# Sparse and forgetting attention written anew: split operands, both token tiles in one bank, rows scaled before the turning

## What is computed

```python
    g = jax.nn.sigmoid(gate.astype(jnp.float32)).reshape(B, T, H, 3)
    o = g[..., 0:1] * o_cmp + g[..., 1:2] * o_slc + g[..., 2:3] * o_win
    return o.astype(h.dtype).reshape(B, T, H * dh) @ w_out
...
    scale = dh ** -0.5
    c = jnp.cumsum(logf, axis=1).transpose(0, 2, 1)
...
        s = jnp.einsum('bqhd,bkhd->bhqk', q[:, lo:hi], k[:, :hi]).astype(jnp.float32) * scale
        s = s + c[:, :, lo:hi, None] - c[:, :, None, :hi]
...
        p = jax.nn.softmax(jnp.where(causal, s, NEG_INF), axis=-1)
        outs.append(jnp.einsum('bhqk,bkhd->bqhd', p.astype(v.dtype), v[:, :hi]))
```

## Time and profile before

| | |
|---|---|
| runs | 3452.91, 3432.66, 3448.34 us; median 3448.34 |
| profiled execution | 3428.43 us, of which the trace's span is 3426.6 |
| busy | PE 3150.3 us (92%), DVE 2056.8 (60%), ACT 1526.5 (45%), POOL 537.9 (16%) |
| chain that ended last | PE 53%, DVE 4%, ACT 1%, POOL 1% |
| granted PE clock, mean | 0.880 of full speed |
| DMA | 134 GB/s over the span, the busiest queue 39.1% of 16 engines |

### The profile page before, as it was taken

How to read it: one execution, slowest core, us unless ns; L and a number is a source line. 1 busy time by engine, 2 the same in 40 slices (tenths; PEclk the granted TensorE clock), 3 DMA queues, 4 the chain that set the end, 5 groups by cost and what they waited for, 6 DMA issues and landing times.

```text
span 3426.6 us, 61848 instructions
## 1 busy us (share of the span) xinstructions
PE 3150.3 (92%) x21774; PEld 2946.0 (86%) x21774; DVE 2056.8 (60%) x4479; ACT 1526.5 (45%) x3283; POOL 537.9 (16%) x590
## 2 busy tenths in 40 slices
PE   7189689999999989798899999999899999999998
PEld 7188679999999867787799999998777799976898
DVE  7948967676776552588676666666422356431465
ACT  5352345555555432423455555554322355531454
POOL 4522680000100110127700000002100010100100
PEclk9589899999999996899999999999655699885799
DMA  4035216666665430352265555554300045430254
GB/s 133 21 113 171 86 55 222 214 231 207 227 225 184 133 111 1 105 173 87 71 220 184 184 183 184 183 184 167 105 1 1 25 144 183 135 104 0 93 184 141
DMA packets 140749, 460.07 MB, mean 134 GB/s; under 512 B 15776, under 2 KB 33568, under 8 KB 140464
## 3 DMA queue, kind: packets, MB, share of 16 engines
q1 hardware_dynamic: 135120, 436.75, 39.1%
q0 software_dynamic: 5472, 21.30, 2.1%
HBM read 448.48 MB, written 9.50 MB: 134 GB/s over the span
## 4 chain that ended last, share of the span: by engine, by line
PE 53%; DVE 4%; ACT 1%; POOL 1%; issue 1%; DVEq 0%; DMA 0%; POOLq 0%; ACTq 0%; SPq 0%
PE banks L769 37%; PE banks L1077 4%; PE banks L1075 3%; PE banks L1096 2%; PE banks L915 2%; PE banks L892 1%; PE banks L1086 1%; PE banks L788 1%; PE banks L1014 1%; POOL x_lo L2012 1%; DVE arena L1667 0%; DVE arena L1680 0%; DVE arena L1633 0%; DVE arena L1626 0%; DVE arena L1627 0%
## 5 line engine op out<-in xcount | busy, mean ns | idle before, releaser
L454 DVE TENSOR_TENSOR w_lo<-ring,w_hi 128x512 fp32r<-128x512 f32 x1464 | 1026.3, 707 | 764.7 <-ACT w_hi L447 758.3
L447 ACT ACTIVATE w_hi<-ring 128x512 fp32r<-128x512 f32 x1464 | 917.9, 631 | 967.1 <-PE banks L769 920.1
L769 PE MATMUL banks<-x_hi,w_hi 128*128 128x256 f32 (+2 forms) x3136 | 913.6, 291 | 57.4 <-POOL x_lo L2012 22.0
L769 PE MATMUL banks<-x_lo,w_hi 128*128 128x256 f32 (+2 forms) x3136 | 905.5, 289 | 0.0
L769 PE MATMUL banks<-x_hi,w_lo 128*128 128x256 f32 (+2 forms) x3136 | 903.1, 288 | 0.0
L769 PE MATMUL banks<-gated_hi,w_hi 128*128 128x256 f32 x2560 | 728.2, 284 | 10.2 <-DVE gated_lo L1760 10.0
L769 PE MATMUL banks<-gated_hi,w_lo 128*128 128x256 f32 x2560 | 727.5, 284 | 0.0
L769 PE MATMUL banks<-gated_lo,w_hi 128*128 128x256 f32 x2560 | 726.2, 284 | 0.0
L769 PEld LDWEIGHTS banks<-x_hi,w_hi 128*128 128x128 f32 x3136 | 613.1, 196 | 67.0 <-issue 40.6
L769 PEld LDWEIGHTS banks<-x_lo,w_hi 128*128 128x128 f32 x3136 | 613.6, 196 | 0.7
L769 PEld LDWEIGHTS banks<-x_hi,w_lo 128*128 128x128 f32 x3136 | 614.0, 196 | 0.0
(11 more groups left out here) (234 smaller groups left out, 3238.9 us busy)
## 6 DMA issues: line engine op xcount, KB each, us to landing
ring<-in_peer_v SPq DMA_DIRECT2D x256, 512.0 KB, 3.5
ring<-in_peer_u SPq DMA_DIRECT2D x192, 512.0 KB, 3.4
arena<-in_peer_u SPq DMA_DIRECT2D x64, 512.0 KB, 3.6
ring<-in_mlp_up SPq DMA_DIRECT2D x64, 512.0 KB, 3.3
ring<-in_mlp_down SPq DMA_DIRECT2D x64, 512.0 KB, 3.3
ring<-w_peer_query SPq DMA_DIRECT2D x32, 512.0 KB, 3.3
ring<-w_fox_proj SPq DMA_DIRECT2D x24, 512.0 KB, 3.4
ring<-w_nsa_proj SPq DMA_DIRECT2D x20, 512.0 KB, 3.4
```

The costliest lines, as they stand in the source:

```text
L447: act.activation(w_hi[:, hn % SPLITS], raw_half(hn), ACT.Copy).then_inc(hi_ready, 1)
L454: dve.tensor_tensor(w_lo[:, hn % SPLITS], raw_half(hn), w_hi[:, hn % SPLITS].bitcast(F32), ALU.subtract)\
L769: mm = pe.matmul(out, w_at(w), x, start=start and j == 0, stop=stop and j == 2, skip_group_check=True)
```

## The change

The attentions of nsa and fox get a new set of functions, `attend_pairs` on four engines and `pair_units`; the first attention (diff) keeps `attend`. A unit is now one head with one set of keys and both token tiles: its scores, 2 x 256 columns, fill one PSUM bank. nsa has 32 such units (8 pairs of heads x 2 x 2 branches), fox 16. q, k, v, masks, decay and the turned probabilities are split into float32r parts. DVE (128 columns) and POOL (256 columns) scale the rows by gate and 1/sum before PE turns them. The values, padded with zeros to 128 columns, are the stationary operand, so the output comes out feature by token and goes split to `x_hi` and `x_lo`; `turn_out` and two barriers per attention are gone, and `proj_keep` waits chunk by chunk. The compressed branch is done for all heads at once, before the first units.

The stages, and PE's part:

```diff
-    ("nsa_attn", dict()),
-    ("turn_out", dict()),
+    ("nsa_attn", dict(joined=True)),
     ("proj_keep", dict(chunks=8, gi=1, squares=NC, joined=True)),
...
+            def attend_pairs(s, units):
...
+                def cmp_scores():
+                    for t in range(NT):
+                        for j in range(8):
+                            o = banks[:, 6, t * SEQ + j * 32:t * SEQ + (j + 1) * 32]
+                            ts = slice(t * P, (t + 1) * P)
+                            for n, (q, k) in enumerate(((q_hi, kc_hi), (q_lo, kc_hi), (q_hi, kc_lo))):
+                                mm = pe.matmul(o, q[:, j, ts], k[:, j // 4], start=n == 0, stop=n == 2, skip_group_check=True)
+                    mm.then_inc(cmp_scored, 1)
...
+                def scores(u):
+                    un = units[u]
+                    if u >= 2:
+                        pe.wait_ge(pair_exp, p0 + u - 1)
+                    o, rows = banks[:, u % 2, :], slice(64 * un["b"], 64 * un["b"] + 64)
+                    pe.matmul(o, ident_r[:, :], mask_r[:, :], start=True, stop=False, skip_group_check=True)
+                    if fox:
+                        sel = ident_r[0:16, un["head"]:un["head"] + 1].broadcast_to([16, P])
+                        for part in range(2):
+                            pe.matmul(o, sel, decay[:, part], start=False, stop=False, skip_group_check=True)
+                    for t in range(NT):
+                        ts = slice(t * P, (t + 1) * P)
+                        for n, (q, k) in enumerate(((q_hi, k_hi), (q_lo, k_hi), (q_hi, k_lo))):
+                            mm = pe.matmul(o[:, t * SEQ:(t + 1) * SEQ], q[rows, un["chunk"], ts], k[rows, un["k"]],
+                                           start=False, stop=t == 1 and n == 2, skip_group_check=True)
...
+                def weigh(u):
+                    pe.wait_ge(pair_lo, p0 + u + 1)
...
+                    for kt, (vh, vl) in enumerate(un["v"]):
+                        at = SEQ if kt == 0 else 0
+                        ph, pl = (pair_pT[:, u % 2, i, at:at + SEQ] for i in range(2))
+                        for n, (v, p) in enumerate(((vh, ph), (vh, pl), (vl, ph))):
+                            mm = pe.matmul(o, v, p, start=first, stop=un["last"] and kt == 1 and n == 2, skip_group_check=True)
...
+                for u in range(len(units) + 3):
+                    if u < len(units):
+                        scores(u)
+                    if u == 2 and not fox:
+                        cmp_turn()
+                    if 2 <= u < len(units) + 2:
+                        turn(u - 2)
+                    if u >= 3:
+                        weigh(u - 3)
```

ACT's order of a unit:

```diff
+                for u in range(len(units) + 4):
+                    if u < len(units):
+                        exps(u)
...
+                    if 2 <= u < len(units) + 2:
+                        round_turned(u - 2)
+                    if u >= 4 and units[u - 4]["last"]:
+                        round_out(u - 4)
```

DVE's:

```diff
+                for u in range(len(units) + 4):
+                    if u < len(units):
+                        maxima(u)
+                    if 1 <= u < len(units) + 1:
+                        scale_rows(u - 1)
...
+                    if 2 <= u < len(units) + 2:
+                        turned_rest(u - 2)
+                    if u >= 4 and units[u - 4]["last"]:
+                        out_rest(u - 4)
```

POOL's:

```diff
+            def attend_pairs(s, units):
+                for u in range(len(units)):
+                    pool.wait_ge(pair_coef, s["p0"] + u + 1)
+                    row = pair_p[:, u % 3, SEQ:2 * SEQ]
+                    pool.tensor_scalar(row, row, pair_coef_[:, u % 3, 1:2], None, ALU.mult).then_inc(pair_scaled_pool, 1)
```

```diff
-        POOL_GROUPS = range(8, GROUPS_OF_TWO)
+        POOL_GROUPS = [g for g in range(8, GROUPS_OF_TWO) if g % 6 != 5]
...
-                    pool.tensor_tensor(hit4, hit4, tk["code"].unsqueeze(2).broadcast_to([P, HEADS, TOPK, NCAND]), ALU.mult)\
-                        .then_inc(hit_ready, 1)
+                    for hd in range(HEADS):
+                        code = tk["code"][:, hd].unsqueeze(1).broadcast_to([P, TOPK, NCAND])
+                        ins = pool.tensor_tensor(hit4[:, hd], hit4[:, hd], code, ALU.mult)
+                    ins.then_inc(hit_ready, 1)
```

More of the change, by code:

```diff
@@ L548, in nsa_rope_dst, with nsa_rope_parts, pair_units @@
         def nsa_rope_dst(m):
-            return qT[:, m] if m < 8 else (kcT, ksT, kwT)[(m - 8) // 2][:, m % 2]
+            return kcT[:, m - 8] if m in (8, 9) else rope_out[:, m % 3]
+        NSA_SPLIT = [m for m in range(14) if m not in (8, 9)]
+        def nsa_rope_parts(m):
+            return (q_hi[:, m], q_lo[:, m]) if m < 8 else (k_hi[:, m - 10], k_lo[:, m - 10])
+        def pair_units(kind):
+            units = []
+            if kind == "fox_attn":
+                for pr in range(8):
+                    for b in range(2):
+                        units.append(dict(chunk=pr, b=b, k=pr, first=b == 0, last=b == 1, head=2 * pr + b,
+                                          v=[(fox_v_hi[:, kt, pr, b], fox_v_lo[:, kt, pr, b]) for kt in range(2)]))
+            else:
+                for j in range(8):
+                    pair = j // 4
+                    for b in range(2):
+                        for i in range(2):
+                            units.append(dict(chunk=j, b=b, k=2 * i + pair, first=b + i == 0, last=b + i == 2,
+                                              gate=3 * (4 * (2 * pair + b) + j % 4) + 1 + i,
+                                              v=[(nsa_v_hi[:, kt, i, pair, b], nsa_v_lo[:, kt, i, pair, b]) for kt in range(2)]))
+            return units
         def block_rows(eng, kv):
@@ L1408, in rope @@
                     follow(split_hi, act, n0 + m)
+                    if beside is not None:
+                        beside(m)
                     act.wait_ge(half_used, 2 * (n0 + m + 1))
```

440 lines of the change are left out of this document (328 added, 112 removed).

## The result

The changed kernel takes 3232.85 us (median of four runs, 3221.49 to 3244.31), beside 3448.32 for the kernel before: ratio 0.9393, 95% interval 0.935 to 0.9435. The forecast was 3223, with a range of 3180 to 3284. On the profiled executions the gain is smaller than on the medians: 3428.43 became 3240.0, where 3202.9 was forecast.

A forecast was written before the change was run, and what follows sets the result against it. PE at half clock was taken to bound nsa's attention. Gains of 123.9 (nsa), 82.6 (fox) and 20 (experts), less 1, make 225.5 us: profiled 3428.4 becomes 3202.9, median 3448.3 becomes 3223, range 3180 to 3284.

The forecast's parts named there:

- the loop over ACT's rounding: New attention units: DVE maxima, ACT exponentials, ACT rounding, DVE rest in turn, 2.82 us; 2.95 nsa, 3.05 fox with output's rest.
- above PE's 2.02 and 2.49 at full clock: New units: the loop outlasts PE's work at full clock, priced at 2.02 us per nsa unit and 2.49 per fox unit.
- The compressed scores: Nsa attention's start: 48 matmuls with new weights at half clock, 48 x 0.214 = 10.3 us.
- I expect it back within the first units, then kept: Both new attentions: PE's clock returns to full within the first units and stays, as new units send more columns per microsecond.
- The ends of 0.8 and 1.2: PE's price for matmuls on 64 and 16 partitions: the full-height price, with ends at 0.8 and 1.2 of it.
- the later casts and shifts of the same tile meet the last pieces, so I take 9: Choice of experts, layer 0: cutting POOL's product into eight pieces gets back 9 us (2 to 11).
- no gain in the choice of experts: Rival: casts meet piece after piece and DVE takes over as bound of the one-hot groups; 3243 us, chance 0.06.
- Half clock: Rival: PE stays at 0.50 in both attentions and ends last, 45 us more, 3268; chance 0.20.
- Held port at the row scaling: Rival: DVE's row scaling in the units waits for POOL's, issued at the same moment; 16 us more, 3239; chance 0.11.
- Serial units: Rival "slower": attention units do not overlap and PE stays at half clock, 8.0 to 8.1 us per unit; 3472; chance 0.03.
- POOL's cover: New units: POOL's scaling of 256 columns, taken as 1.1 us, is hidden with some 1.5 us of cover before ACT's rounding.
- nothing in the change bears on that distance: Whole kernel: the profiled execution lies 19.9 us below the runs' median, and this distance was carried over unchanged.

The follow-up runs named there:

- experiment 1: Changed kernel with ACT rounding the turned piece of the unit two back before this unit's exponentials, not behind them; ratio 0.9375 to the kernel before.
- experiment 8: Changed kernel with DVE scaling all 384 columns, POOL's scaling and PE's wait for it gone; nsa 112.1 us, fox 73.7 us.
- experiment 4: Changed kernel with 40 matmuls of 512 columns into an unread bank filling PE's wait at the start of the compress stage; ratio 0.9409.
- experiment 10: Changed kernel with ACT's rounding first and fox's two decay matmuls per unit left out; fox 46.4 us, its full-clock units 2.34 us on average.
- experiment 5: Kernel before with only POOL's product in the choice of experts cut into eight pieces; 3422.65 us in one run.
- experiment 6: Kernel before with only the POOL one-hot groups cut from 120 to 100; 3429.53 us in one run, groups 120.9 and 120.1 us.
- experiment 2: Changed kernel with POOL's row scaling doubled by an extra multiplication by 1.0; nsa 119.1 us against 112.5, fox units 3.08 against 2.985.
- experiment 3: Changed kernel with 18 matmuls of 512 columns into an unread bank ahead of fox's first scores; fox 56.8 us against 60.7.

## Why the prediction was right, and where it missed

**Who sets the pace.** Right in nsa, not in fox. In nsa the loop over ACT's rounding was named from the order and priced from rows of before at 2.95 us; measured 2.80. The 0.1 between the 2.82 of the sum and 2.72 is mostly overlap on DVE: the rest (L2156) is recorded with 0.56 us, but what stands behind it starts after 0.48, and the output's rest, recorded with 0.41, adds 0.33. Experiments 1 and 8 show that in nsa it is this loop: cut, the units get shorter; with POOL and PE's wait for it taken out, they stay. In fox "above PE's 2.02 and 2.49 at full clock" failed: PE's 2.99 is above the loop's 2.89 and ends last. That the units came out near the 3.05 of the forecast is luck there.

**Nsa.** -128.6 against -127.5. Two errors cancel: 28 units 0.15 shorter each (4 us less), and the first units longer, 16.8 us to the fifth maximum where 14.4 stood. The compressed scores took 10.2 us (2499.61 to 2509.84), as summed at half clock. By the page's rule (the Trainium skill, TensorE: Matmul & The Clock Gate, LDWEIGHTS) it would have been 5. The traces agree with it at full clock and not at half: matmuls of 60 columns with new weights each start 0.11 us apart at 1.00 (experiment 4, 2432.70 to 2434.49) and 0.21 apart at 0.50.

**Fox.** -76.9 against -85.2. The failing step is the clock, "I expect it back within the first units, then kept". It came back 22 us into the stage, after five units, in the other kernels after 13 to 54 us. At half clock a unit is 5.26 us, where 4.56 stood. Up to the fourth maximum it took 14.4 us where 8.7 stood, and the next two units 9.5 where 6.1 stood; the eleven at full clock gave 0.7 back. The second failing step is PE's price of a fox unit, 2.49: it is 2.99 (experiments 1 and 10), because two decay matmuls on 16 partitions cost 0.65 and not 0.47, and a change of shape costs PE 0.1 each time. PE's timeline of the changed kernel shows both, in fox units at full clock (the turnings 2.99 and 2.98 us apart; the decay's two start 0.66 us before the first score, that 0.22 before the second, and the second 0.12 before the third):

```profile
2975.39 0.55 PE L1132 MATMUL banks<-const_a,arena 128*128 128x128 f32 x3
...
2976.81 0.72 PE L1118 MATMUL banks<-decay,ident_r 16*128 16x512 f32 x2
2977.47 0.38 PE L1122 MATMUL banks<-k_hi,q_hi 64*128 64x256 f32 x1
2977.69 0.28 PE L1122 MATMUL banks<-k_hi,q_lo 64*128 64x256 f32 x1
2977.81 0.28 PE L1122 MATMUL banks<-k_lo,q_hi 64*128 64x256 f32 x1
...
2978.38 0.55 PE L1132 MATMUL banks<-const_a,arena 128*128 128x128 f32 x3
...
2981.36 0.55 PE L1132 MATMUL banks<-const_a,arena 128*128 128x128 f32 x3
```

The ends of 0.8 and 1.2 stood for the matmuls on 64 and 16 partitions alone. These are 1.18 of the unit's 2.49, so 1.2 of them would make it 2.73: 2.99 lies outside.

**Compress, both projections.** +3.4, +2.0 and +2.1 against +3.6, +1 and +2.6: right.

**Choice of experts.** -12.4 against -20. The step that failed: "the later casts and shifts of the same tile meet the last pieces, so I take 9", and "3" in layer 1. They were 6.3 and -0.2, in the changed kernel and in experiment 5 alike (layer 0 counted from PE's first score matmul, as told there): a hold of 12 us on one operation became holds of 1.7 on several. The groups gave 6.2 of 8 (experiment 6). The rival "no gain in the choice of experts" had the right mechanism and went too far.

**Rivals.** Half clock: false for both attentions as a whole, true for the first five fox units, and the clock returned in nsa with the fifth. Held port at the row scaling: false (DVE's took 0.29 us in every unit). Serial units: false.

**POOL's cover.** The forecast gave 1.5 us; it is 0.8 (experiment 2). It cost nothing in the changed kernel, but once the loop was cut it ended last in two of four nsa units.

**The distance to the median.** "nothing in the change bears on that distance" was right by its words and wrong in use. The profiled execution of before had the short diff attention, that of after the long one. The profiled execution missed its 3202.9 by 37.1 us: 21.9 are diff, 15.2 the rest (8.3 fox, 7.6 the experts, the others 0.7 the other way). The medians are over runs that differ by about 20 us on both sides, and miss by 9.9; that this is so little owes something to luck.

## What to carry to other kernels

Cut a loop over two in-order engines by asking which of the two orders is free: moving one operation ahead of its neighbour gave 0.32 us per nsa unit with no work saved. It gave nothing in fox, where PE ended last at full clock: ask that first. When you size the cover of an operation, follow what stands behind its waiting reader on that engine, not only the reader. And cutting a long blocking operation into pieces helps one victim; if several short operations stand behind each other, each meets a piece of its own.

## What the runs showed of the hardware

- POOL's product of two inputs held DVE's casts, shifts, two-input products and scaled one-hots until the piece ended (0.23 us became 1.66 to 1.76, with the whole product 12.58), while DVE's sum over 6400 columns ran beside it in 6.80 us, its length of before (6.81). The Trainium skill (VectorE: DVE Perf Modes, Mode 2×_2P) says that in this mode, open only to operations with one tensor source in SBUF, both read ports fetch that one tensor; together with the shared port named in the prediction this agrees with the casts, says nothing of the two-input products, and does not agree with the next point.
- POOL's one-input operations did not hold DVE's: in the one-hot groups of the kernel before, 232 of DVE's scaled one-hots started while POOL was building one, and took 0.34 us (median, 0.40 at most), the same as the 40 others. So it is the kind of POOL's operation that decides, with DVE's the same: 0.34 us beside a scaling, 1.75 beside the product. On DVE a scaling takes 0.29 us for 128 columns and 0.35 for 256, on POOL 0.70 to 0.76 and 1.02.
- Eight pieces of the product took 13.6 to 14.3 us together, the whole 12.6.
- The clock: at 0.50 in diff attention for 65 to 143 us in kernels that had not changed there, with PE busy 65.00 of 65 us before and 128.53 of 143 in the changed kernel. It fell in a stretch of 60-column matmuls in which PE did not pause (experiment 4), and inside a wait of 1.37 us (experiment 3). The length of the half-clock stretch in diff likely makes most of the 20 us between runs of one kernel. What decides it was not found.
